# The first tile's opening of a two-layer decoder trunk, rebuilt: coefficients on VectorE, attention in batches, the merge in sections

## The chip, the cores and the metric

The kernel runs on one core of a Trainium2 chip. The metric is the time of one execution in device microseconds, as the median of several. Times inside the kernel come from one profiled execution, counted from its first instruction. DVE is VectorE, ACT is ScalarE, PE is TensorE (PEld its weight loads), POOL is GpSimd, SP is SyncE, which issues the plain DMAs; a DMA indexed by a tensor (a gather) is issued by GpSimd.

## What is computed

Two layers over 256 tokens of width 1024, float32. Each layer has a token mixer and a retrieval over single-neuron experts:

```python
h = rms_norm(x, g1); q, k, v, f, u_pool, u_ssm = split(h @ w_in)
att  = forgetting_attention(q, k, v, f)   # 8 heads x 64, q and k normalised, bias from cumsum(log_sigmoid(f))
pool = multiscale_pool(u_pool)            # windows 2, 4, 8, 16, then 64x64 products
ssm  = s5_mixer(u_ssm)                    # a_bar = exp(a*dt) complex, b_bar = (a_bar-1)/a*b, scan over time,
                                          # y = gelu(.), y * sigmoid(y @ glu_w + glu_b)
x = x + concat(rms_norm(att), rms_norm(pool), rms_norm(ssm)) @ w_out
h2 = rms_norm(x, g2)                      # PEER: for each of 8 heads, from h2 @ w_q:
                                          # top 16 of 128 keys, twice; top 16 of the 256 sums; softmax -> gates
act = gelu(h2 . u[expert])                # 128 experts a token
x = x + sum(gate * act * v[expert])
```

The outputs are the 256x1024 rows after both layers.

## The kernel before

Tokens are taken in tiles of 128, one token to a partition. Two tiles and two layers make four steps, n = 0 to 3 (n = 0 and 1 are the tiles of the first layer). In each step a token needs 128 expert rows (u and v side by side, 8 KB); expert E of all 128 tokens is one gather of 1 MB into one of 12 slots (`slot`). VectorE makes the dot product of u with h2 (`dots`), ScalarE the Gelu and, for each expert, a diagonal matrix with gate times Gelu (`weigh`), and TensorE adds diagonal times v into PSUM (`add_last`, one group behind). Four experts are a quad; a step has 32 quads. A gather into a used slot waits for `expert_done`.

Everything else is cut into pieces with names, and one list, `ORDER`, is walked by every engine, which takes from each name its own part. `MIX0` is the order ahead of the first gather: the whole mixer of step 0 up to its first routing head (`route0`), and of step 1 the projections up to q, k, v (entries `("qkv0", 1)`). Behind it `script()` deals rows of pieces to the quads: `ROUTES` (heads 1 to 7 of step 0) and `MIX1` (the rest of step 1's mixer and its eight routing heads) to the quads of step 0, and `MIX` with `ROUTES` of step n+1 to those of step n. `route` is, on VectorE, the top-16 work of one head, ending with the indices (`idx`, semaphore `routed`) and, after ScalarE's exponential, the gates.

The pieces that matter here: `dt`, `inverse`, `tab0` to `tab3` make the discretised coefficients of the state space model, on GpSimd, for one layer at a time: a Taylor polynomial (`exp_start`), nine squarings (`exp_double`), and `coefficients`; `tab4` makes the input matrices (`b_bar`), `rotate0` to `rotate2` tables of powers over time (for layer 1 on GpSimd, `tab5` to `tab7`). `bu`, `scan`, `backA`, `backB`, `y`, `z`, `glu` are the model itself: drive products, turning them by the powers, 16 scans along time, turning back, output, Gelu (here from Tanh on ScalarE and products on VectorE), gate. `qkn` normalises q and k, `qkT` transposes and scales them; `att0` to `att4` do two heads each: logits on TensorE into one half bank a head, `max` and `nrm` (maximum, and division by the sum) on VectorE for each head alone, exponential and copies on ScalarE. `attT`, `mixT` copy results out of PSUM, `sq`, `merge` compute the three norms together and `out0` to `out3` are the output projection; `x1` adds the residual.

The weights come in chunks of 1 MB. Those of step 0 up to `out3` lie in the 12 slots that later take experts; step 1 uses the same chunks for its projections, so a first gather waits until its slot's chunk is used by both. The other chunks pass through a ring of two buffers: chunk c is loaded when chunk c-2 is used, and the second buffer is scratch of step 0's model until `s_ready`.

## Time and profile before

| | |
|---|---|
| median of 3 runs | 1639.59 us (1638.54 to 1640.44) |
| profiled execution | 1639.44 us, span 1637.6 us |
| DVE busy | 1116.6 us (68%) |
| PE busy | 1079.0 us (66%) |
| POOL busy | 665.4 us (41%) |
| ACT busy | 431.1 us (26%) |
| DMA | 623.52 MB, of them 536.90 MB by gathers, mean 381 GB/s |
| mean granted TensorE clock | 0.825 of full speed |

The first gather is issued at 145.18 us. A busy share is a mean over stages that have different limits, so it says little by itself. The DMA row of the page has the mean busy share of the 16 DMA engines in 40 equal slices of 41 us; in the windows one sees the same for chosen stretches.

### The profile page before, as it was taken

The page shows a single profiled execution, that of the slowest core. Times are in us where ns is not written, and L with a number is a line of the kernel's source. Part 1 is how long each engine was busy: PE and PEld are TensorE (multiplying, and loading weights), DVE is VectorE, ACT ScalarE, POOL GpSimd, SP SyncE. Part 2 cuts the span into 40 slices and gives each one's busy share as a digit, 9 for nine tenths or more (in the row PEclk, how much of TensorE's full clock was granted, in tenths as well). Part 3 has the DMA queues.
Part 4 walks back from the last instruction along what each step waited for, and adds up shares of the span by engine and source line. Part 5 has one row for each costly group of instructions (what it writes and reads, how often), then busy time and mean ns, then how long its engine had stood idle before and what let it go on. Part 6 is the DMA issues. An engine that isn't in the chain of part 4 may idle for free. (4 is left out here: it accounts for less than half of the span.)

```text
span 1637.6 us, 19577 instructions
## 1 busy us (share of the span) xinstructions
PE 1079.0 (66%) x6936; PEld 560.8 (34%) x6936; DVE 1116.6 (68%) x2614; ACT 431.1 (26%) x1118; POOL 665.4 (41%) x793
## 2 busy tenths in 40 slices
PE   7795665777576576676677586667766656555654
PEld 6665331442343143332254243434244311111111
DVE  3833999755599957666379968656469975455455
ACT  2221332341233320234033331225133321111111
POOL 6002333685285344334433353344333354444431
PEclk9998786988788688888888797888878876787688
DMA  9005999979999899999999999999999999999997
GB/s 392 22 30 224 419 419 358 420 308 399 397 419 390 353 419 419 420 419 420 420 382 420 419 412 420 419 419 419 420 392 419 414 372 420 420 419 420 419 419 319
DMA packets 86067, 623.52 MB, mean 381 GB/s; under 512 B 9809, under 2 KB 9809, under 8 KB 10961
## 3 DMA queue, kind: packets, MB, share of 16 engines
q0 software_dynamic: 73728, 536.90, 79.8%
q1 hardware_dynamic: 12240, 85.37, 12.8%
q8 instruction: 54, 0.88, 0.2%
q14 instruction: 45, 0.36, 0.1%
HBM read 621.19 MB, written 1.05 MB: 380 GB/s over the span
## 5 line engine op out<-in xcount | busy, mean ns | idle before, releaser
L455 POOL DMA_INDIRECT slot<-experts,idx x512 | 570.5, 1114 | 928.6 <-PE acc L1348 722.4
L1038 DVE CUSTOM_DVE_ANT_0 slot<-slot,h 128x1024 f32<-128x1024 f32 x512 | 616.4, 1230 | 348.8 <-DMA slot<-experts,idx 337.5
L1348 PE MATMUL acc<-slot,diag 64*64 64x512 f32 x4080 | 612.3, 751 | 366.3 <-ACT diag L732 365.6
L1348 PEld LDWEIGHTS acc<-slot,diag 64*64 64x64 f32 x4080 | 179.2, 168 | 745.4 <-ACT diag L732 442.0
L732 ACT ACTIVATE diag<-cst,ge 128x64 f32<-128x64 f32 x510 | 136.2, 336 | 149.1 <-DVE ge L758 133.8
L723 ACT ACTIVATE ge<-ge 128x4 f32<-128x4 f32 x129 | 26.5, 206 | 475.5 <-DVE ge L1038 474.6
L1315 PE MATMUL PB<-hT,ring 128*128 128x128 f32 x1024 | 129.8, 289 | 14.1 <-DMA ring<-weights 9.8
L1315 PEld LDWEIGHTS PB<-hT,ring 128*128 128x128 f32 x1024 | 126.2, 205 | 16.7 <-issue 10.9
L723 ACT ACT_TABLE_LOAD x56 | 71.8, 1283 | 28.4 <-DVE ge L1038 27.5
L716 ACT ACTIVATE rs<-bs 128x1 f32<-128x1 f32 x32 | 6.5, 203 | 235.0 <-DVE bs L973 227.6
L1288 PE MATMUL PX<-ring,work 128*128 128x512 f32 x96 | 51.5, 686 | 16.7 <-DVE work L948 16.7
L1163 PE MATMUL PB<-ring,hT 128*128 128x256 f32 x192 | 51.8, 430 | 14.9 <-DVE work L758 14.9
L758 DVE TENSOR_TENSOR ge<-ge,gate 128x4 f32<-128x4 f32 x129 | 21.1, 164 | 48.4 <-ACT ge L723 17.5
L1163 PEld LDWEIGHTS PB<-ring,hT 128*128 128x128 f32 x192 | 40.8, 218 | 28.7 <-DVE work L758 16.6
L1038 DVE DVE_READ_ACCUMULATOR2_ANT ge<- 128x1 f32 x512 | 41.7, 82 | 0.0
L425 POOL TENSOR_TENSOR base<-base 128x16 f32<-128x16 f32 (+1 forms) x138 | 39.1, 301 | 4.6
L717 ACT ACT_TABLE_LOAD x31 | 39.8, 1283 | 0.6
L1288 PEld LDWEIGHTS PX<-ring,work 128*128 128x128 f32 x96 | 20.0, 219 | 48.0 <-issue 28.7
L668 ACT ACT_TABLE_LOAD x14 | 18.0, 1283 | 53.7 <-DVE att_s L922 53.6
L1299 PE MATMUL PB<-cst,h 128*128 128x128 f32 x32 | 7.2, 390 | 32.9 <-DVE h L962 32.8
L1213 PE MATMUL PX<-kT,qTz 128*128 128x128 f32 (+1 forms) x64 | 19.7, 396 | 11.1 <-DVE kT L909 11.1
L1324 PEld LDWEIGHTS PB<-ring,work 128*128 128x128 f32 x128 | 16.7, 190 | 26.3 <-issue 24.9
(227 smaller groups left out, 1143.7 us busy)
## 6 DMA issues: line engine op xcount, KB each, us to landing
ring<-weights SPq DMA_DIRECT2D x32, 1152.0 KB
ring<-weights SPq DMA_DIRECT2D x28, 1024.0 KB
slot<-weights SPq DMA_DIRECT2D x12, 1024.0 KB, 21.7
slot<-experts,idx POOLq DMA_INDIRECT x512
sml<-small SPq DMA_DIRECT2D x2, 1160.0 KB, 11.1
xs<-x SPq DMA_DIRECT2D x2, 512.0 KB, 7.8
out<-xs SPq DMA_DIRECT2D x4, 256.0 KB
cst<-consts SPq DMA_DIRECT2D x1, 564.5 KB, 4.7
```

The source lines that it names most:

```text
L425: return pool.tensor_tensor(o, a, b, op)
L455: pool.indirect_dma_start(out=slot[:, E % SLOTS, :], out_offset=None, in_=src, in_offset=bass.IndirectOffsetOnAxis(ap=idx[:, n % 2, e:e + ...
L717: told(act.activation(bs[:, 1, :], bs[:, 0, :], ACT.Exp, bias=rs[:, 0:1], accum_out=rs[:, 1:2]), "gexp_ready")
L723: act.activation(ge[:, 1, G % 2, :], ge[:, 0, G % 2, :], ACT.Gelu_apprx_tanh).then_inc(S["gelu_ready"], 1)
L732: act.activation(diag[:, d % DIAGS, :], c_("fold"), ACT.Copy, scale=ge[:, 2, G % 2, i:i + 1]).then_inc(S["diag_ready"], 1)
L758: return dve.tensor_tensor(o, a, b, op)
L1038: ins = dve.tensor_tensor_reduce(u, u, h2[:, n % 2, :], 1.0, 0.0, ALU.mult, ALU.add, d[:, i:i + 1])
L1163: ins = pe.matmul(PB[:, bank, (i % 2) * 256:(i % 2) * 256 + 256], hT_(n)[:, k, :], c[:, k, :], start=(k == 0), stop=(k == KD - 1))
L1213: pe.matmul(o, qTz[:, t, h // 2, h % 2, :], kT[:, h // 2, 0:w], start=True, stop=False)
L1288: ins = pe.matmul(PX[:, half, :], W[0][:, k * P:k * P + P], c[:, (k % 2) * D + half * 512:(k % 2) * D + half * 512 + 512], start=(k == 0), ...
L1315: ins = pe.matmul(PB[:, 2 + h % 2, i * P:i * P + P], c[:, k, i * P:i * P + P], hT[:, k, :], start=(k == 0), stop=(k == KD - 1))
L1348: ins = pe.matmul(acc[HALF * half:HALF * half + HALF, i, :], diag[rows, d % DIAGS, :], slot[rows, E % SLOTS, D + half * 512:D + half * 512 ...
```

## The change

`MIX0` is rewritten. The coefficients of both layers are made at once on VectorE (`power0` to `power2`, 16 columns instead of 8, imaginary part and real part in one operation where it goes), from a small table of their own (`factors`); `dt`, `inverse` and `tab0` to `tab3` of layer 1 disappear from step 0, where only `tab4` to `tab7` are left to GpSimd. Attention of step 0 is done in two batches of four heads (`logits`, `big`, `even`, `turn`, `pv`), the scan in three parts between them, norms and merge in three sections, pooling first, then attention, then the model (`sq1 merge1`, `sq0 merge0`, `sq2 merge2`), with the output chunks in the order 2, 0, 1, 3; results are read from PSUM without a copy. Gelu is one function of ScalarE. Queries lie unpadded in `qT`. The projections q, k, v of step 1 stand behind `route1`, and their normalisation and transposes are the first rows of the quads; `route1` is in `MIX0`. Experts go to slots in another order (`place`), the output chunks' slots first. In all steps the exponential of a routing head (`soft`) stands on ScalarE behind the quad's diagonals instead of ahead of them, and the product of Gelu and gate is four copies with a scale on ScalarE instead of one VectorE operation.

The core of the diff (places in PSUM and SBUF, renamings and packing on the host are left out):

```diff
-MIX0 = ("normA", "dt", "inverse", "tab0", "tab1", "tab2", "tab3", "tab4",
-        "normT", "u", "uT", "pf", "gate", "ln", "cum", ("normA", 1), "qkv0", "qkv1", ("normT", 1),
-        "rotate0", "qkv2", "qkv3", "qkn", "rotate1", "qkv4", "qkv5", "bT", "qkT", "v", "rotate2", "bu", "att0",
-        ("pf", 1), ("gate", 1), "pool", "max0", "scan", "nrm0", "mixp", "att1", ("u", 1), "backA", "mixT", "max1", ("ln", 1),
-        ("qkv0", 1), "backB", "nrm1", ("uT", 1), "att2", "max2", "y", "nrm2", ("qkv1", 1), "z", "att3",
-        "max3", "glu", ("cum", 1), "nrm3", ("qkv4", 1), "att4", "attT", "sq", "merge", ("qkv2", 1), ("qkv3", 1),
-        ("qkn", 1), "out0", "out1", "out2", ("qkT", 1), "out3", ("qkv5", 1), "x1", ("v", 1), "h2T", "rp",
-        "route0")
-MIX1 = (("bu",), ("scan",), ("backA",), ("backB",), ("y", "z"), ("glu", "pool", "dt", "inverse"),
-        ("att0", "max0", "nrm0"), ("att1", "max1", "nrm1", "mixp", "mixT"), ("att2", "max2", "nrm2", "tab0"),
-        ("att3", "max3", "nrm3", "tab1"), ("att4", "attT", "sq", "tab2"), ("merge", "tab3"),
+MIX0 = ("normA", "dt", "inverse", "normT", "u", "power0", "power1", "pf", "uT", "gate", "ln", "power2", "tab4",
+        "rotate0", "cum", ("normA", 1), "qkv0", "qkv1", "rotate1", ("normT", 1), "bT", "qkv2", "rotate2", "bu",
+        "qkv3", "qkn0", "scan0", "qkv4", "qkn1", "qkv5", "v", "qkT", "scan1", "logits0", "big0", "scan2", "logits1",
+        "big1", ("u", 1), "pool", "even0", ("pf", 1), "backA", ("uT", 1), "turn0", "even1",
+        ("gate", 1), "mixp", "pv0", "turn1", "backB", "pv1", ("ln", 1), "sq1", "merge1", "y", "z", ("cum", 1), "sq0", "merge0",
+        "glu", "out2", "out0", "out1", "sq2", "merge2", "out3", "x1", "h2T", "rp", "route0", "soft0",
+        "route1", "soft1", ("qkv0", 1), ("qkv1", 1), ("qkv2", 1), ("qkv3", 1), ("qkv4", 1), ("qkv5", 1))
+MIX1 = (("bu",), ("scan",), ("backA",), ("backB",), ("y", "z"), ("glu", "pool"),
+        ("att0", "max0", "nrm0"), ("att1", "max1", "nrm1", "mixp"), ("att2", "max2", "nrm2"),
+        ("att3", "max3", "nrm3"), ("att4", "sq"), ("merge",),
...
-            rows = [(0, r) for r in ROUTES] + [(1, r) for r in MIX1]
+            rows = [(1, r) for r in ((), ("qkn",), ("qkT", "v"))]
+            rows += [(0, r) for r in ROUTES[1:]] + [(1, r) for r in MIX1]
...
+            for step, row in rows[done:at]:
+                order += [("mix", "soft" + s[5:], step) for s in row if s[:5] == "route"]
...
+def place(E):
+    return (E + CH_OUT) % SLOTS
...
+def merged_by(n, i):
+    return 4 * n + ((2, 3, 1, 4)[i] if n == 0 else i + 1)
+def normed(n, sec=2):
+    return sec_order(sec) if n == 0 else 3 + n
+def sec_order(sec):
+    return (2, 1, 3)[sec]
...
                 if c == 1:
                     sp.wait_ge(S["s_ready"], 1)
+                    sp.wait_ge(S["chunk_used"], uses(0, CH_OUT + 2))
...
                     if E < SLOTS:
-                        pool.wait_ge(S["chunk_used"], max(uses(0, E), uses(1, E) if in_slot(1, E) else 0))
-                        pool.wait_ge(S["qkT_ready"], 2)
+                        i = place(E)
+                        pool.wait_ge(S["chunk_used"], max(uses(0, i), uses(1, i) if in_slot(1, i) else 0))
...
-                if part == 0:
-                    exp_start(l)
-                elif part == 1:
-                    exp_double(l, HALVINGS // 2)
-                elif part == 2:
-                    exp_double(l, HALVINGS - HALVINGS // 2)
-                elif part == 3:
-                    coefficients(l)
-                elif part == 4:
+                if part == 4:
                     b_bar(l)
...
+                    return
+                if part == 5:
+                    pool.wait_ge(S["states_ready"], TILES)
+                rotate(l, tt, lag, link, W[1], ((1, 2, 4, 8, 16), (32,), (64,))[part - 5])
...
+                act.preload_act_table_set("natural_log_exp_and_others")
+                told(act.activation(step[:, :], tabc[:, 2, :], ACT.Exp), "dt_ready")
...
+                act.preload_act_table_set("natural_log_exp_and_others")
...
-                told(act.activation(gl[:, 1, :, :], gl[:, 0, :, :], ACT.Tanh, scale=GELU_S), "gtanh_ready")
+                told(act.activation(gl[:, 0, :, :], gl[:, 2, :, :], ACT.Gelu_apprx_tanh), "z_ready")
...
+            def logits(n, a):
+                act.wait_ge(S["nmax_ready"], 4 * a + 4)
+                for i in range(4):
+                    at = 4 * a + i
+                    told(act.activation(W[2][:, at * P:at * P + P], PX[:, a, i * P:i * P + P], ACT.Exp,
+                                        bias=att_s[:, 0, at:at + 1], accum_out=att_s[:, 1, at:at + 1]), "exp_ready")
+            def turn(n, a):
+                act.wait_ge(S["probT_psum"], 4 * a + 4)
+                told(act.copy(W[2][:, a * 512:a * 512 + 512], PB[:, a, :]), "probT_ready", 4)
...
+            def sq(n, sec=None):
...
+            def merge(n, sec=None):
+                act.wait_ge(S["norm_psum"], normed(n, 2 if sec is None else sec))
+                cols = slice(0, 3 * P) if sec is None else slice(sec * P, sec * P + P)
+                told(act.activation(rB[:, :, :].rearrange("p a b -> p (a b)")[:, cols], norm_at(n)[:, cols], ACT.Sqrt,
                                bias=eps), "norm_rms")
...
+            def soft(n, h):
+                R = PH * n + h
                 act.wait_ge(S["top_ready"], R + 1)
                 link(act.activation(rs[:, 0:1], bs[:, 0, 0:1], ACT.Copy, scale=-1.0))
                 told(act.activation(bs[:, 1, :], bs[:, 0, :], ACT.Exp, bias=rs[:, 0:1],
...
+                if quad % PER_HEAD == 0 and quad < QUADS:
+                    act.wait_ge(S["gated"], PH * n + quad // PER_HEAD + 1)
+                for i, E in enumerate(mine):
+                    e = E - PICKS * n
+                    ins = act.activation(ge[:, 2, G % 2, i:i + 1], ge[:, 1, G % 2, i:i + 1], ACT.Copy,
+                                         scale=gate[:, n % 2, e:e + 1])
+                told(ins, "w_ready")
...
+            def power(n, part):
+                if part == 0:
+                    dve.wait_ge(S["zeroed"], 1)
+                    dve.wait_ge(S["dt_ready"], 1)
+                    lag(stt(zz[:, 0, 0, :], tabc[:, 0, :], 0.5 ** HALVINGS, step[:, :], ALU.mult, ALU.mult))
+                    link(stt(zz[:, 1, 1, :], tabc[:, 1, :], 0.5 ** HALVINGS, step[:, :], ALU.mult, ALU.mult))
...
+                    for k in range(TERMS - 1, 0, -1):
+                        lag(stt(A, Z, 1 / k, U[:, 0, :].unsqueeze(1).to_broadcast(wide), ALU.mult, ALU.mult))
+                        link(stt(B, Z, 1 / k, U[:, 1, :].unsqueeze(1).to_broadcast(wide), ALU.mult, ALU.mult))
+                        lag(stt(U[:, 0, :], A[:, 0, :], 1.0 if k > 1 else 0.0, B[:, 1, :], ALU.add, ALU.subtract))
+                        link(tt(U[:, 1, :], A[:, 1, :], B[:, 0, :], ALU.add))
+                elif part == 1:
+                    for i in range(HALVINGS):
+                        x, y = ((U, A), (A, U))[i % 2]
+                        p, q = ((U, B), (B, U))[i % 2]
+                        lag(stt(A[:, 0, :], x[:, X[i % 2], :], 2.0, x[:, X[i % 2], :], ALU.add, ALU.mult))
+                        lag(stt(B[:, 0, :], p[:, 1, :], 4.0 ** i, p[:, 1, :], ALU.mult, ALU.mult))
+                        lag(stt(q[:, 1, :], x[:, X[i % 2], :], 1.0, p[:, 1, :], ALU.add, ALU.mult))
+                        link(tt(y[:, X[1 - i % 2], :], A[:, 0, :], B[:, 0, :], ALU.subtract))
+                else:
+                    R, pr, pi = ta[:, 1, 0, :], ta[:, 1, 1, :], tb[:, 1, 1, :]
...
+                    e = ta[:, 0, :, :]
+                    pair = [P, 2, LSB]
+                    lag(tt(uu[:, 0, :, :], e, tabc[:, 0, :].unsqueeze(1).to_broadcast(pair), ALU.mult))
+                    link(tt(tb[:, 0, :, :], e, tabc[:, 1, :].unsqueeze(1).to_broadcast(pair), ALU.mult))
+                    lag(tt(drive_c[:, 0, :], uu[:, 0, 0, :], tb[:, 0, 1, :], ALU.add))
+                    link(tt(drive_c[:, 1, :], uu[:, 0, 1, :], tb[:, 0, 0, :], ALU.subtract))
...
+            def scan(n, part=3):
...
+                if part % 3 == 0:
+                    link(tt(w3[0], w3[0], spare, ALU.add))
+                    link(tt(w3[1], w3[1], w3[3], ALU.subtract))
+                for r in ((), (0,), (1,), (0, 1))[part]:
...
-                link(dve.tensor_scalar(gl[:, 0, :, :], gl[:, 0, :, :], GELU_C, 1.0, ALU.mult, ALU.add))
-                told(tt(gl[:, 0, :, :], gl[:, 0, :, :], y, ALU.mult), "garg_ready")
-            def z(n):
-                gl = gl_(n)
-                y = gl[:, 2, :, :]
-                dve.wait_ge(S["gtanh_ready"], n + 1)
-                told(dve.scalar_tensor_tensor(gl[:, 0, :, :], gl[:, 1, :, :], 1.0, y, ALU.add,
-                                         ALU.mult), "z_ready")
+                told(ins, "yd_ready")
...
-                qp, kp = (b.rearrange("p (a b) -> p a b", a=PAIRS) for b in qk_banks(n)[1:])
-                for o in range(2):
-                    r = slice(64 * o, 64 * o + 64)
-                    link(dve.tensor_scalar(qTz[r, t, :, o, :], qp[r], s_("qg")[r], DH ** -0.5, ALU.mult, ALU.mult))
...
+                link(dve.tensor_scalar(qT[:, t, :, :], qp, s_("qg"), DH ** -0.5, ALU.mult, ALU.mult))
...
+            def big(n, a):
+                dve.wait_ge(S["logits_psum"], 4 * a + 4)
+                told(dve.tensor_reduce(att_s[:, 0, 4 * a:4 * a + 4], PX[:, a, :].rearrange("p (h k) -> p h k", h=4), AX.X,
+                                       ALU.max, negate=True), "nmax_ready", 4)
+            def even(n, a):
+                dve.wait_ge(S["exp_ready"], 4 * a + 4)
+                link(dve.reciprocal(att_s[:, 2, 4 * a:4 * a + 4], att_s[:, 1, 4 * a:4 * a + 4]))
+                x = W[2][:, a * 512:a * 512 + 512].rearrange("p (h k) -> p h k", h=4)
+                told(tt(x, x, att_s[:, 2, 4 * a:4 * a + 4].unsqueeze(2).to_broadcast([P, 4, P]), ALU.mult),
+                     "prob_ready", 4)
...
-            def attT(n):
-                dve.wait_ge(S["pv_psum"], HEADS * (n + 1))
-                told(dve.tensor_copy(h2[:, n % 2, 0:512], PB[:, 2, :]), "attT_ready")
...
+            def merge(n, sec=None):
+                dve.wait_ge(S["norm_rms"], normed(n, 2 if sec is None else sec))
+                secs = slice(0, 3) if sec is None else slice(sec, sec + 1)
+                link(dve.reciprocal(rB[:, secs, :], rB[:, secs, :]))
+                for k in range(KD) if sec is None else BLOCKS[sec]:
...
-                        ins.then_inc(S["merged_ready"], 1)
-                dve.wait_ge(S["merged_ready"], 4 * (n + 1))
+                        told(ins, "merged_ready")
...
-                if G >= 2:
-                    dve.wait_ge(S["diag_ready"], by_tensor(experts_of(*divmod(G - 2, QUADS))[-1] + 1))
-                told(tt(w, ge_(1, n, quad), gate[:, n % 2, mine[0] - PICKS * n:mine[-1] + 1 - PICKS * n], ALU.mult),
-                     "w_ready")
...
+                    pe.wait_ge(S["hT_ready"], 4)
+                if n == 1:
+                    pe.wait_ge(S["v_ready"], 2)
+                    pe.wait_ge(S["qkT_ready"], 2)
...
                 if n == 1 and i == 0:
-                    pe.wait_ge(S["up_ready"], 2)
-                    pe.wait_ge(S["fx_ready"], 2)
-                if n == 1 and i == 2:
-                    pe.wait_ge(S["attT_ready"], 1)
+                    pe.wait_ge(S["x1_ready"], 1)
                 if n == 1 and i == 4:
-                    pe.wait_ge(S["sig_ready"], 1)
-                bank = qk_banks(n)[0] + i // 2
+                    pe.wait_ge(S["h2T_ready"], 2)
...
+            def logits0(n, a):
...
+                for i in range(4):
+                    one_head(n, 2 * i + a, PX[:, a, i * P:i * P + P], P)
+            def turn0(n, a):
+                pe.wait_ge(S["prob_ready"], 4 * a + 4)
+                for i in range(4):
+                    at = 4 * a + i
+                    ins = pe.transpose(PB[:, a, i * P:i * P + P], W[2][:, at * P:at * P + P], ident)
+                ins.then_inc(S["probT_psum"], 4)
+            def pv0(n, a):
+                pe.wait_ge(S["probT_ready"], 4 * a + 4)
+                if a == 0:
+                    pe.wait_ge(S["uT_ready"], 2)
+                for i in range(4):
+                    h, at = 2 * i + a, 4 * a + i
+                    ins = pe.matmul(PB[DH * a:DH * a + DH, 2, i * P:i * P + P], V[:, 0, h * DH:(h + 1) * DH],
+                                    W[2][:, at * P:at * P + P], start=True, stop=True)
+                ins.then_inc(S["pv_psum"], 4)
...
+            def merge(n, sec=None):
+                pe.wait_ge(S["sq_ready"], normed(n, 2 if sec is None else sec))
+                if n == 0 and sec != 1:
+                    pe.wait_ge(S["norm_rms"], normed(n, sec) - 1)
+                for i in range(3) if sec is None else (sec,):
+                    sq = sq_at(n, i)
...
+                pe.wait_ge(S["merged_ready"], merged_by(n, i))
+                if n == 0:
+                    pe.wait_ge(S["exp_ready"], HEADS)
```

## Rows read from the trace of the kernel before

**Rows 1.** Page, part 2: what DMA moved in 40 equal slices.

```profile
GB/s 392 22 30 224 419 419 358 420 308 399 397 419 390 353 419 419 420 419 420 420 382 420 419 412 420 419 419 419 420 392 419 414 372 420 420 419 420 419 419 319
```

**Rows 2.** Waits: who waited for whom, us in total, times, longest.

```profile
POOL slot L455 <- DVE idx L1010: 106.4, 1, 106.4
```

**Rows 3.** Windows: length, busy us and instructions by engine, clock, DMA.

```profile
core 0: us, PE busy (x) PEld busy (x) DVE busy (x) ACT busy (x) POOL busy (x), PEclk, DMA share, GB/s
260.00:300.00 40.00, 23.25 (x162) 7.43 (x163) 38.58 (x71) 5.63 (x22) 19.88 (x16) 0.75 0.94 376
340.00:380.00 40.00, 24.74 (x148) 12.61 (x148) 22.00 (x44) 12.71 (x30) 33.20 (x67) 0.80 0.78 295
500.00:580.00 80.00, 47.30 (x312) 20.86 (x312) 73.83 (x198) 29.14 (x69) 36.20 (x34) 0.77 0.93 370
900.00:1265.00 365.00, 252.26 (x1680) 134.46 (x1680) 262.01 (x600) 110.49 (x275) 138.60 (x124) 0.83 1.01 416
```

**Rows 4.** Timeline, from the residual to the first indices: start, length, instruction.

```profile
123.82 1.22 DVE L758 TENSOR_TENSOR xs<-xs,PX 128x1024 f32<-128x1024 f32 x1 [1.11 <-PE PX L1288]
...
144.71 0.17 DVE L1010 SCALAR_TENSOR_TENSOR idx<-ex 128x16 uint32<-128x16 f32 x1
```

**Rows 5.** Groups by form, 0 to 145 us: busy us, mean ns, idle before.

```profile
L1163 PE MATMUL PB<-slot,h 128*128 128x256 f32 x96 | 22.6, 391 | 0.8 <-ACT ring L629 0.8
L1163 PE MATMUL PB<-slot,hT 128*128 128x256 f32 x96 | 21.2, 380 | 0.0
...
L1288 PE MATMUL PX<-slot,work 128*128 128x512 f32 x32 | 14.1, 592 | 0.0
...
L1112 PE MATMUL PB<-slot,h 128*128 128x256 f32 x16 | 5.4, 510 | 5.8 <-DVE work L758 5.8
...
L1112 PE MATMUL PX<-slot,hT 128*128 128x256 f32 x16 | 3.6, 379 | 0.0
```

**Rows 6.** Windows of VectorE's work on the tile rot: length, busy, instructions.

```profile
32.00:40.00 8.00, 6.86 (x31) 1.00 1.02 420
43.00:46.00 3.00, 2.10 (x6) 1.00 0.06 25
49.00:53.20 4.20, 3.70 (x6) 1.00 0.01 4
```

**Rows 7.** Timeline of the opening, six kinds of work on VectorE and GpSimd.

```profile
33.28 0.27 DVE L758 TENSOR_TENSOR work<-rot 128x8 f32<-128x8 f32 x2
...
34.24 2.88 POOL L425 TENSOR_TENSOR ring<-tabp,base 128x256 f32<-128x256 f32 x4
...
37.20 1.53 POOL L425 TENSOR_TENSOR ring<-ring 128x256 f32<-128x256 f32 x2
...
55.96 2.48 DVE L758 TENSOR_TENSOR work<-PB,rot 128x1024 f32<-128x1024 f32 x2
...
61.64 5.16 DVE L846 TENSOR_TENSOR_SCAN work<-base,work 128x128 f32<-128x128 f32 x16
...
103.45 2.55 DVE L943 RECIPROCAL rB<-rB 128x384 f32<-128x384 f32 x1 [6.64 <-ACT rB L686]
```

**Rows 8.** Timeline of ScalarE around one table load.

```profile
25.07 1.28 ACT L613 ACT_TABLE_LOAD   x1
...
26.37 0.40 ACT L613 ACTIVATE work<-work,cst 8x128 f32<-8x128 f32 x1
```

**Rows 9.** Timeline of one quad with a routing head, late in step 0.

```profile
507.59 1.22 DVE L1038 CUSTOM_DVE_ANT_0 slot<-slot,h 128x1024 f32<-128x1024 f32 x1
...
512.29 0.49 DVE L969 MAX8 ts<-work 128x8 f32<-128x128 f32 x2
...
514.33 3.74 PE L1315 MATMUL PB<-hT,ring 128*128 128x128 f32 x32
...
520.73 1.06 ACT L732 ACTIVATE diag<-cst,ge 128x64 f32<-128x64 f32 x4 [0.70 <-DVE ge L758]
```

**Rows 10.** Timeline of GpSimd: first and last of 108 arithmetic instructions.

```profile
316.51 0.12 POOL L472 MEMSET base<- 128x8 f32 x1
...
370.24 0.24 POOL L521 TENSOR_SCALAR base<-base 128x8 f32<-128x8 f32 x1
```

More of the change, by code:

```diff
@@ L733, in weigh @@
                                    scale=ge[:, 2, G % 2, i:i + 1]).then_inc(S["diag_ready"], 1)
-            run(dict(dt=dt, normA=normA, gate=gate, ln=ln, bT=turn_b, z=z, glu=glu, qkn=qkn, v=v, att=att, pool=pool_, sq=sq,
-                     merge=merge, x1=x1_, h2T=h2T, rp=rp, route=route), lambda n, quad: None, weigh)
+            run(dict(dt=dt, normA=normA, gate=gate_, ln=ln, bT=turn_b, z=z, glu=glu, qkn=qkn, v=v, att=att, pool=pool_, sq=sq,
+                     logits=logits, turn=turn,
+                     merge=merge, x1=x1_, h2T=h2T, rp=rp, route=route, soft=soft), lambda n, quad: None, weigh)
         @block.vector
```

447 lines of the change are left out of this document (218 added, 229 removed), and 4 rows, old and new, of the table MIX.

## The prediction

> **What bounds the kernel now.** I read the slices of the page first. What DMA moves is near 420 GB/s in all slices but numbers two to four: the queue is busy for the first 40 us, almost empty until the gathers begin, and then full to the end [rows 1]. So the kernel is an opening of 145 us with little traffic and 1,490 us of expert rows. Only two things can change the time: when the first gather is issued, and how much DMA stands still later. The waits say the first: GpSimd's gather waits 106.4 us, once, for the first indices [rows 2]. The windows of 40 us say the second [rows 3]; a loss is the GB/s missing to 420, over 420, times the length. 260 to 300 loses 4.2 us, 340 to 380 loses 11.9, 500 to 580 loses 9.5; 900 to 1265 stands for the rest with 1%. The losses look different: at 260 to 300 and 500 to 580 VectorE is busy 96 and 92% of the time, at 340 to 380 only 55%, while GpSimd has 67 instructions and 33 of 40 us.
>
> **The opening.** Today the first indices are written at 144.88 [rows 4]. Twelve q, k, v chunks of TensorE stand ahead of that; the six of tile 1, 22.6 us, leave [rows 5]. VectorE loses there tile 1's key and query normalisation and scaling and much waiting between heads. What is left has to be laid on the engines anew.
>
> *To 22.2 us.* Nothing changes until the first tile's hT at 11.5. Then VectorE raises the powers in 67 narrow operations. Two such take 0.27 together [rows 7]; with pipelining I take 0.1 for one that waits only for the one before last and 0.2 for one whose own end is awaited: 3.0 us (10 and 10), 4.5 (27 and 9) and 1.5 (7 and 4), with 1.6 for uT between them. GpSimd then has only the B matrices left, 4.5 us as today (34.24 to 38.73 [rows 7]), to 26.8.
>
> *To 51.6.* rotate0 takes 7.3 as now, 31 operations, of them 6.86 busy, beside GpSimd [rows 6]; cum, normA and hT 0.7, 0.9 and 1.45; rotate1 and rotate2 2.1 and 3.9 [rows 6]: 38.6. Turning the drive: four operations of 1.24 [rows 7], 43.6. Then qkn's reduction, two sums and qkn's product, again over 1024 columns: 5.3, to 48.8. TensorE's own sum, with six chunks of 3.65 (between the 3.53 and 3.77 of the rows), ends at 48.7, a tie; from here a slower TensorE costs one for one. Transposes 1.1 and two scalings 1.5: 51.6.
>
> *To 68.1.* VectorE: sixteen scans 5.2 [rows 7], two maxima over 512 columns 1.3, even0 and even1 0.85 each, backA and backB 3.7 and 4.1, uT 0.4: 68.1. TensorE meanwhile: logits 3.9, u of tile 1 3.9, pool 0.8, pf of tile 1 5.5, so the batched turn starts at 65.8, 7 us after its probabilities, and the last value product ends at 69.8. Both arms end within 2 us.
>
> *To 91.2.* Here ScalarE's tables set the pace. merge1's root costs 1.28+0.28; VectorE stands before it until 72.9, then does 1.5 (a third of the 2.55 reciprocal [rows 7] and two products of 0.3). y 0.6; Gelu 1.28+0.42, to 76.9; squares 0.6, norm sum 0.7 and glu product 1.2, to 79.5; a root and a tanh, each behind its load, to 81.8; glu 0.4; out0 and out1 1.75 each (0.44 for a 512-column matmul [rows 5]), to 85.7, out2 being hidden. The last section: sum 0.4, root 1.56, merge2 1.5, out3 1.75, with 0.3 of hand-overs 91.2. From x1 to the indices the chain is today's: 123.82 to 144.88, 21.1 us [rows 4]. Sum 112.4.
>
> **TensorE's clock.** Rows show what a restart costs: pf's 16 matmuls took 5.4 us after 5.8 us of idling and 3.6 without it [rows 5], 1.8 us. The new order has sparse work before out2. I add one such restart (bounds: pf itself warm, 110.6; three, 117.8) and forecast the first indices at 114: 31 us earlier, bounds 27 and 34.
>
> The trace shows a table load as 1.28 us with 0.02 to its operation [rows 8]. The Trainium skill, "ScalarE: Activation LUTs", section "What ACT_TABLE_LOAD costs", puts about 1.38 us of drain on top of each switch, and that speaks against this change. By that figure the five switches on the chain would make 114 into 121. The rows show no such time, and I take none.
>
> **The head start behind it.** On TensorE the second tile's q, k, v now stand behind route1, and gathers 6 to 11 need those chunks' slots. TensorE comes to them some 1 us after the indices and frees one each 3.65: at +4.6 up to +22.9. DMA needs 2.5 us a gather (1 MB at 420 GB/s), and has six free ones, 5.6 us of landing latency and two weight chunks ahead: gather 11 is served at about +35. This cover is 12 us; without it each us is one of DMA. Behind the waiting gather on GpSimd's queue stand only later gathers. SP's second ring chunk now also waits for out2, at 81, and is needed at 105. route1 on VectorE, 8.2 us (512.29 to 520.5 [rows 9]), moves out of the crowded stretch to where VectorE waits for the first expert.
>
> **Step 0 after that.** (a) GpSimd's arithmetic for layer 1, 108 instructions from 316.51 to 370.48 [rows 10], is gone; it stood in blocks of 6 to 12 us before groups of four gathers that carry 10 us. VectorE has room there: -12 (bounds -13, and -5 if another engine limits). (b) 260 to 300: VectorE now lacks route1's 8.2 and gets tile 1's normalisation, 5.0: -4.2 (bounds that and 0). (c) At the end of step 0, 34 rows are dealt to 32 quads; eight routes fall on seven quads, the last with two. A quad with a route is 4.9+8.2 on VectorE (dots from 507.59, maxima from 512.29 [rows 9]) against 12.8 on DMA (4 MB and 1.15 MB of weights): eight routes in eight quads leave VectorE 2.5 us short (105 for 102.4), eight in seven 7.5 (99.9 for 92.4). In return diagonals no longer wait for the route's end: they come at 520.73 though the dots end at 512.25, and could come at 515.5; TensorE's other work ends at 518.07 [rows 9], so slots are free 3 us sooner, each time, and VectorE may fall 3 us further behind. In the last quad the exponential of route6 stands behind route7's copy and comes some 4 us late. Net 5+4-3 = +6 (bounds -4, where the 3 us count in every quad and the 4 not, and +10).
>
> (d) Four small ScalarE copies, 0.2 us each like its narrow operations, replace one VectorE product of a quad. ScalarE is 26% busy (the table), so they are hidden while slots come in time. In steps 1 to 3 I take 0 (bounds -4 and +5). At the very end one dependent operation more: +0.2.
>
> **Sum.** The profiled execution took 1639.4 (span 1637.6; median of the runs 1639.6): 1639.4-31-12-4.2+6+0.2 = 1598.4.
>
> **Rivals.**
> *Only the opening pays*: 340 to 380 was spare, and the crowded end takes all back: 1639.4-31 = 1608.4. For it: VectorE at 92% in 500 to 580 [rows 3]. Against: 45% of room at 340 to 380. 0.20.
> *The opening is a chain of hand-overs* that costs 8 more, indices at 122: 1606.4. For it: some 20 hand-overs between 68 and 91, and the restart's row. Against: today's hand-overs, 0.1 each, are in my sum. 0.12. By the skill's drain alone, part of this case, it would be 1605.3, 0.04 of it.
> *Slots come sooner everywhere*: (c) is -4 and the later steps give 3: 1585.4. For it: the 3 us of earlier diagonals. Against: throughput of VectorE, not latency, limits there. 0.14.
> *Slower.* One mechanism: the route's exponential stands on ScalarE behind the quad's diagonals, and the third of these waits for TensorE's products. Gelu, copies and diagonals end about 3.9 us after the dots, the exponential at 6.4, VectorE wants it at 7.7: 1.3 us in hand. If it is later than that by 2.9 us at each of the 14 routes of step 0, where VectorE is the limit, 41 us are lost and the gain is gone; at 3.2 the time is 1643. Against: TensorE is ahead, its products for the next quad's route ran from 514.33 [rows 9], 11 us before VectorE's maxima could use them. 0.02.
> *The change does nothing*, another wait holding the first gather: 1639, 0.01. The forecast itself: 0.51.
>
> **The numbers.** 1598.4 is the likeliest, its own range 1592 to 1604. Terms' bounds and the rivals' reach give 1586 to 1611 for eight in ten. What a measurement can tell from no change here is 0.2%, 3.3 us. Faster 0.96, same 0.015, slower 0.025.
>
> **What would show it.** Right: the first gather near 114; the powers' operations ending near 22; pf of tile 1 straight ahead of the batched turn; five table loads between 71 and 88; no dip at 300 to 350, one at the end of step 0. Wrong: the first gather before 108 or after 120; gathers 6 to 11 issued after DMA ran dry; VectorE waiting for ScalarE's exponential in each route; the dip of 340 to 380 back under another releaser.

## The result and the profile after

The changed kernel took 1617.77 us (median of 4 runs, 1612.66 to 1619.6) against 1640.01 for the kernel before: ratio 0.9857, 95% interval 0.9835 to 0.988. I had forecast 1598.4 with a range of 1586 to 1611. It is faster, as said, but by little more than half of what was said.

The profiled execution's span is 1614.6, 23.0 less. This splits at the first indices. Waits of the changed kernel (who waited for whom, us in total, times, longest):

```profile
POOL slot L521 <- DVE idx L1097: 117.0, 2, 113.7
ACT rs L750 <- DVE bs L1060: 30.8, 29, 6.4
```

and its timeline at the first indices (start, length, instruction):

```profile
141.12 0.17 DVE L1097 SCALAR_TENSOR_TENSOR idx<-ex 128x16 uint32<-128x16 f32 x1
```

They come at 141.29. Before it was 144.88 [rows 2, 4]: only 3.6 us earlier, where I forecast 31. The other 19.4 us came behind the opening, where I forecast 10.0. Both halves were wrong, in opposite directions. The split is good to some 2 us only: one profiled execution stands for each kernel, and six kernels below that keep the old opening (e6, e7, e8, e11, e12, e13) have their first indices between 142.3 and 143.4.

**Where the opening lost it.** My working held to within 1.7 us as far as the scaled queries and keys (ready at 51.6 by the sum; the first logit starts at 53.34). Then the timeline of TensorE shows the first head of the batched logits, the first product of the fifth, and what follows the eighth:

```profile
53.34 0.48 PE L1299 MATMUL psum<-kT,qT 64*128 64x128 f32 x2 [1.70 <-DVE kT L991]
53.76 0.49 PE L1300 MATMUL psum<-cT,cst 128*128 128x128 f32 x2
54.08 0.39 PE L1301 MATMUL psum<-cst,cT 128*128 128x128 f32 x2
54.31 0.39 PE L1302 MATMUL psum<-cst 128*128 128x128 f32 x2
...
60.91 0.79 PE L1299 MATMUL psum<-kT,qT 64*128 64x128 f32 x2
...
69.97 0.42 PE L1185 MATMUL psum<-h,slot 128*128 128x128 f32 x1
```

The first head takes 1.28 us, the second 1.7, the later ones 2.30, and all eight 16.6 (53.34 to 69.97) where I had put 3.9. The windows of 5 us (columns as in [rows 3]) show why they change in mid-stream:

```profile
50.00:55.00 5.00, 2.75 (x18) 2.19 (x18) 3.67 (x9) 0.00 (x0) 0.00 (x0) 1.00 0.01 3
...
65.00:70.00 5.00, 5.00 (x20) 4.10 (x20) 0.00 (x0) 0.00 (x0) 0.00 (x0) 0.50 0.00 0
...
90.00:95.00 5.00, 0.00 (x0) 0.00 (x0) 2.92 (x7) 2.52 (x5) 0.00 (x0) 0.50 0.00 0
95.00:100.00 5.00, 4.71 (x18) 4.15 (x19) 0.79 (x1) 2.73 (x4) 0.00 (x0) 0.52 0.00 0
```

The granted clock is 1.00 at 50 and down to 0.50 from about 55.5 to 72, with TensorE busy all the time from the first logit on. Before the logits it had idled twice, 1.24 us ahead of the transposes and 1.70 behind them. It falls again at 90 to 100, this time behind idling. From the merge to the routing the timeline has:

```profile
95.29 2.08 PE L1396 MATMUL psum<-work,cst 128*128 128x128 f32 x8 [5.40 <-ACT work L696]
...
98.86 4.06 PE L1407 MATMUL psum<-slot,ring 128*128 128x512 f32 x8
102.76 7.03 PE L1407 MATMUL psum<-slot,work 128*128 128x512 f32 x16
...
113.74 5.23 PE L1407 MATMUL psum<-slot,work 128*128 128x512 f32 x8 [3.50 <-DVE work L1036]
```

Two output chunks are 16 instructions and 7.03 us, so one is 3.5. I had read [rows 5] as 1.75.

**Where the rest gained.** Windows from the first indices to the end of each step, the kernel before first, then the changed one:

```profile
144.00:566.00 422.00, 267.13 (x1776) 137.54 (x1775) 331.19 (x861) 127.77 (x316) 223.71 (x297) 0.81 0.96 387
566.00:947.00 381.00, 254.55 (x1716) 136.50 (x1720) 271.28 (x640) 111.72 (x282) 141.73 (x127) 0.84 1.01 415
947.00:1325.00 378.00, 262.44 (x1760) 140.34 (x1752) 272.81 (x640) 113.66 (x284) 145.22 (x130) 0.83 1.00 411
```

```profile
141.00:556.00 415.00, 279.72 (x1874) 154.31 (x1872) 326.59 (x822) 151.70 (x441) 195.61 (x191) 0.83 0.98 402
556.00:928.00 372.00, 255.32 (x1724) 135.34 (x1724) 264.09 (x606) 138.66 (x412) 146.05 (x128) 0.84 1.00 415
928.00:1305.00 377.00, 267.38 (x1748) 143.27 (x1748) 265.34 (x599) 140.55 (x412) 143.80 (x128) 0.83 1.01 416
```

Step 0 was 33 us short of a full queue (422 times 33/420) and is now 20 short (415 times 20/422). Step 1's 9 us are no better use of the queue, 415 both times: bytes moved from it into step 0, whose transfers run further ahead. And the full rate itself is another: 419 to 420 GB/s in [rows 1], here mostly 421:

```profile
GB/s 391 30 30 239 422 420 422 407 315 422 411 420 420 357 412 422 421 420 421 421 392 421 421 421 421 421 416 420 421 382 421 421 411 421 421 421 421 422 421 310
```

What is new in step 0 is one dip. Windows of the changed kernel around it, and GpSimd's next gather in its timeline:

```profile
260.00:300.00 40.00, 20.84 (x124) 5.79 (x116) 39.28 (x67) 9.28 (x31) 18.87 (x15) 0.70 1.01 421
320.00:340.00 20.00, 13.12 (x53) 7.92 (x56) 9.22 (x23) 6.17 (x19) 1.49 (x2) 0.57 0.62 258
340.00:380.00 40.00, 30.58 (x229) 15.47 (x222) 24.64 (x46) 23.05 (x62) 21.37 (x20) 0.95 0.98 398
```

```profile
339.43 0.94 POOL L521 DMA_INDIRECT slot<-experts,idx  x1 [18.51 <-PE psum L1463]
```

The gather waits 18.5 us for a slot, at clock 0.57, while the second tile's attention begins. The dip of [rows 3] at 260 is gone, and that at 340 nearly (398 GB/s for 295).

### The profile page after: what moved, and what is told of

Read it like the earlier page. It is cut to its first block and busy times, and to the rows that moved or that the text cites. A ratio compares the mean times of both kernels' runs of the same rounds, so it can differ in the third digit from the quotient of the medians.

```text
span 1614.6 us, 19582 instructions
## 1 busy us (share of the span) xinstructions
PE 1089.5 (67%) x6936; PEld 570.1 (35%) x6936; DVE 1091.3 (68%) x2504; ACT 539.2 (33%) x1626; POOL 626.1 (39%) x577
## 5 line engine op out<-in xcount | busy, mean ns | idle before, releaser
L1463 PE MATMUL psum<-slot,diag 64*64 64x512 f32 x4080 | 598.4, 736 | 319.5 <-ACT diag L773 312.4
L1463 PEld LDWEIGHTS psum<-slot,diag 64*64 64x64 f32 x4080 | 175.1, 165 | 689.4 <-ACT diag L773 371.7
L1430 PE MATMUL psum<-hT,ring 128*128 128x128 f32 x1024 | 136.7, 298 | 24.1 <-DMA ring<-weights 18.7
L1430 PEld LDWEIGHTS psum<-hT,ring 128*128 128x128 f32 x1024 | 132.9, 214 | 27.2 <-issue 20.2
L764 ACT ACTIVATE ge<-ge,gate 128x1 f32<-128x1 f32 x512 | 109.0, 283 | 4.2
L1407 PE MATMUL psum<-ring,work 128*128 128x512 f32 x96 | 50.5, 675 | 18.1 <-DVE work L1036 18.1
L1245 PE MATMUL psum<-ring,hT 128*128 128x256 f32 x192 | 50.9, 424 | 12.3 <-DVE work L803 12.3
L1245 PEld LDWEIGHTS psum<-ring,hT 128*128 128x128 f32 x192 | 40.1, 215 | 25.9 <-DVE work L803 14.1
L1407 PEld LDWEIGHTS psum<-ring,work 128*128 128x128 f32 x96 | 19.6, 216 | 49.0 <-issue 28.3
L1439 PE MATMUL psum<-ring,work 128*128 128x128 f32 x128 | 23.3, 306 | 9.3 <-ACT work L736 9.3
L1439 PEld LDWEIGHTS psum<-ring,work 128*128 128x128 f32 x128 | 17.1, 194 | 33.8 <-issue 19.7
```

What stands on the lines that cost most here:

```text
L764: ins = act.activation(ge[:, 2, G % 2, i:i + 1], ge[:, 1, G % 2, i:i + 1], ACT.Copy, scale=gate[:, n % 2, e:e + 1])
L1245: ins = pe.matmul(bank[:, (i % 2) * 256:(i % 2) * 256 + 256], hT_(n)[:, k, :], c[:, k, :], start=(k == 0), stop=(k == KD - 1))
L1407: ins = pe.matmul(PX[:, half, :], merged(n, k), c[:, (k % 2) * D + half * 512:(k % 2) * D + half * 512 + 512], start=(k == (4 if n == 0 el ...
L1430: ins = pe.matmul(PB[:, 2 + h % 2, i * P:i * P + P], c[:, k, i * P:i * P + P], hT[:, k, :], start=(k == 0), stop=(k == KD - 1))
L1439: ins = pe.matmul(PB[:, 2 + h % 2, 256 + i * P:256 + i * P + P], qTs[:, h % 2, i * P:i * P + P], raw[:, KD * 256 + i * P:KD * 256 + i * P ...
L1463: ins = pe.matmul(acc[HALF * half:HALF * half + HALF, i, :], diag[rows, d % DIAGS, :], slot[rows, place(E), D + half * 512:D + half * 512 ...
```

## Experiments on the opening

Median, ratio to the kernel before with its 95% interval, end of the first indices in the profiled execution. The kernels were run in groups at different times, each beside runs of the kernel before (whose medians were 1638.4 to 1641.4), so between groups the ratios are the better comparison.

| kernel | us | ratio | indices |
|---|---|---|---|
| changed | 1617.8 | 0.9857 (0.9835 to 0.988) | 141.3 |
| e1: grouped by shape | 1610.5 | 0.9831 (0.9815 to 0.9848) | 134.4 |
| e2: padded queries | 1608.7 | 0.9826 (0.9809 to 0.9842) | 132.2 |
| e3: before, unpadded | 1639.2 | 1.0004 (0.999 to 1.0018) | 143.8 |
| e4: grouped, v in the gap | 1615.3 | 0.9857 (0.9841 to 0.9873) | 140.0 |
| e9: padded, kept warm | 1599.2 | 0.9762 (0.9729 to 0.9795) | 124.9 |
| e10: e9, two pieces moved | 1597.5 | 0.9738 (0.9717 to 0.9759) | 124.1 |

**e1, logits grouped by shape.** Here and in e4 the sums of four heads are open in one bank at the same time, and the values are left out of account; only the time counts.

```
-for i in range(4): one_head(n, 2 * i + a, PX[:, a, i * P:i * P + P], P)
+for i in range(4): matmul(o[i], qT[rows, 0, i], kT[rows, i, 0:P], start=True)   # 64 rows
+for i in range(4): the three 128-row matmuls of head 2 * i + a
```

> The changed kernel, but in the batched logits the four products of 64 rows (query by key) of a half come first and the twelve of 128 rows (decays and mask) behind them, so that TensorE changes between the two shapes twice in place of eight times. Theory 1, the changes of shape make the logits long (16.6 us for 8 heads, where the kernel before took 0.88 us a head) and the clock falls because of them: the logits take 5 to 7 us, the first indices come 9 to 12 us earlier (129 to 132 us) and the time is 1606 to 1609. Theory 2, the clock falls by itself at this place and the change of shape is cheap: the logits stay over 12 us and the time within 2 us of the changed kernel's 1617.8. Theory 3, the opening's end is set by something else (SP's or POOL's queue): logits shorter, indices still at 141.

**e2, padded queries.** `qTz[P, TILES, PAIRS, 2, P]`, zeroed once, and two scalings as in the kernel before; the product reads `qTz[:, t, h // 2, h % 2, :]` and `kT[:, h // 2, 0:w]`.

> The changed kernel with the queries padded with zeros to 128 rows, as in the kernel before, so that every product of the logits has 128 rows; the order within a head is that of the changed kernel. Costs one VectorE operation more after the transposes (about 0.5 us). Theory 1, the changes of shape are the cost: logits 5 to 7 us, first indices at 129 to 133, time 1606 to 1610, and steps 1 to 3 change by a microsecond at most, since attention there is hidden. Theory 2, not the shape but the batching or the clock: logits over 12 us and the time at 1617 to 1620.

e2 has its logits in 7.2 us, its indices at 132.2 and 1608.7 us: theory 1, with the logits a little over its 5 to 7. e1 (logits 9.4 us, 54.67 to 64.09; 134.4; 1610.5) goes theory 1's way but misses its three ranges by 1.5 to 2.4 us. The timeline of TensorE in e2, the first head, a later one, and what follows:

```profile
54.46 0.49 PE L1302 MATMUL psum<-kT,qTz 128*128 128x128 f32 x2 [2.49 <-DVE kT L994]
54.78 0.39 PE L1303 MATMUL psum<-cT,cst 128*128 128x128 f32 x2
...
60.81 0.39 PE L1302 MATMUL psum<-kT,qTz 128*128 128x128 f32 x2
...
61.70 3.74 PE L1188 MATMUL psum<-h,slot 128*128 128x128 f32 x32
```

A head is 0.90 us to the last, the clock stays at 1.00, and the first indices come 9.1 us earlier. The time is 9.1 us lower by the medians and 5.1 by the two ratios. In e1 the clock fell too, but came back within the batch. The 5 us from 55 on, in e1, in e2 and in e10 (padded as well, described below):

```profile
55.00:60.00 5.00, 5.00 (x31) 4.78 (x30) 2.28 (x8) 0.00 (x0) 0.00 (x0) 0.66 0.00 0
```

```profile
55.00:60.00 5.00, 5.00 (x47) 5.00 (x46) 3.60 (x11) 0.75 (x4) 0.00 (x0) 1.00 0.00 0
```

```profile
55.00:60.00 5.00, 5.00 (x33) 5.00 (x32) 2.01 (x6) 0.00 (x0) 0.00 (x0) 0.66 0.00 0
```

So padding doesn't rule the fall out. The idle times ahead of the batch were 1.70 us in e1, 2.49 in e2, and in e10 2.49 with another 1.23 ahead of the transposes; e10's logits took 8.9 us (53.85 to 62.73). What lets the clock fall at this place, idling or the 64-row products, stays open. What the three have against the changed kernel is that the clock was at 1.00 again from 59 on, while there, with the two shapes alternating, it stayed at 0.50 to the end of the batch.

**e3, the kernel before with unpadded queries alone.** `qT` for `qTz`, one scaling for two, `qT[rows, t, h // 2, :]` in the product.

> The kernel before with only its queries unpadded (64 rows in the query by key product, one VectorE operation less), the rest of the change left out. Theory 1: a head's four products go from 0.88 us to 1.3 to 2.3 us, eight of them +3 to +11 us on TensorE, of which the waits between heads hide a part: first indices 2 to 6 us later than 144.9 and the time 1642 to 1646. Theory 2, the shape is cheap: 1639 to 1641 and a head at 0.9 us.

Theory 2 on the time, theory 1 on the price of a head. A head is now 1.28 us (in the timeline the first starts at 49.68 and the second at 50.96), 0.38 more than padded, but at full clock, two heads at a time, with waits of TensorE between the pairs that hide it. The same edit is free in the old order and costs 9 us of the first indices in the batch.

**e4, v of the second tile in TensorE's gap.** Grouped logits, and `("qkv4", 1), ("qkv5", 1)` ahead of the pooled section's sum of squares.

> As the grouped logits, and the second tile's v (two of its six projections and the copy) is moved from behind the first tile's routing into TensorE's idle stretch ahead of the merge. Theory A, the cold clock in the merge (0.5 granted between 90 and 100 us) costs some 4 to 6 us and work in the gap keeps it up: indices 2 to 5 us earlier than with the grouped logits alone, time 1601 to 1606. Theory B, the filled work only stands in front of the merge: indices the same or 1 to 2 us later, time within 2 us of the grouped kernel's.

Theory B, and worse than it said: 4.8 us slower than e1, indices 5.5 later. The attention section's sum of squares starts at 92.59 where e1 has 88.20, so the two chunks stand in front of the merge; the clock falls all the same further down (the last output chunk 6.57 us, the first routing product 6.75). This doesn't settle what the clock costs; the next run does.

**e9, padded and kept warm.**

```
+def warm(n, times):
+    for i in range(times):
+        pe.matmul(PB[:, 1, :], ident, cst[:, 0:512], start=True, stop=True)
 ... "pv1", "warm2", ... "y", "z", "warm5", ... "merge2", "warm3", "out3", "warm4", "x1"
```

> The changed kernel with padded queries, and 14 products of 128 by 512 whose result nobody reads, in four places where TensorE stands idle in the opening (2 behind the last value product, 5 behind the state output, 3 behind the third sum of squares, 4 behind the last output projection; 0.88 us each at full clock). With padded queries alone the first indices came at 132.1, and three stretches ran at half clock: the first heads' sum of squares 2.07 us, the last output projection 5.36, the first routing product 6.23. Theory A, the falls of the clock cost their sum, 1.2 + 1.8 + 2.5 = 5.5 us: those three at 0.9, 3.6 and 3.8 us, indices at 126 to 128, time 1602 to 1605. Theory B, the products stand in the way or the clock falls all the same: indices at 131 to 134 and the time within 2 us of 1608.7.

Theory A, and more: 7.3 us, not 5.5. In the timeline of e9 the three that ran cold (2.07, 5.36 and 6.23 us in e2) are

```profile
85.37 1.16 PE L1403 MATMUL psum<-work,cst 128*128 128x128 f32 x8 [1.02 <-ACT work L697]
...
101.67 3.70 PE L1414 MATMUL psum<-slot,work 128*128 128x512 f32 x8 [0.92 <-DVE work L1039]
...
111.55 3.84 PE L1437 MATMUL psum<-hT,ring 128*128 128x128 f32 x32 [0.73 <-ACT hT L727]
```

with the granted clock at 1.00 in every window from 45 to 125. They make 5.0 of it. The glu product (1.06 for 1.92), the first output chunk (3.60 for 4.31) and the transposes (1.44 for 1.89) make 2.0 more, and e9's logits started 0.4 us earlier than e2's, which its edit doesn't explain. So the warm clock is worth 7.0.

**e10, e9 with two pieces moved.** `("ln", 1), ("cum", 1)` to behind `"out1"`, `"sq2", "merge2"` ahead of it, `"warm2"` and `"warm3"` dropped. Nine unread products are left, not the 11 of the text below.

> The changed kernel with padded queries, 11 of the 14 unread products, and two pieces of the opening moved: the second tile's forget gate (a ScalarE table load of 1.28 us and two activations, and VectorE's scan) from ahead of the pooled section's root to behind the last sum of squares, and the gated section's sum of squares ahead of the second attention projection in place of behind it. Worked out from the padded and warmed run: its root, reciprocal and scaling (4.1 us after the sum) come to lie beside a projection of 3.5 us, -3.3, and the pooled section's squares no longer wait 2.0 us for the gate, -2. Theory A, the opening is one chain: indices at 119 to 121 in place of 124.9, time 1593 to 1596. Theory B, what is moved is replaced by the next waits: indices at 123 to 125 and the time within 2 us of 1599.2.

Theory B by both numbers (124.1, and 1.7 us below e9), though something did move: the last output chunk ends at 101.7, 3.7 us earlier than in e9 (of 5.3 expected), but the first indices come only 0.8 earlier. The timeline of e10:

```profile
104.26 1.28 ACT L583 ACT_TABLE_LOAD   x1
105.56 0.29 ACT L583 ACTIVATE st<-st,cst 128x1 f32<-128x1 f32 x1
...
109.13 5.47 PE L1437 MATMUL psum<-hT,ring 128*128 128x128 f32 x32 [0.73 <-ACT hT L727]
```

The gate's logarithm, moved behind the last root, leaves another table on ScalarE, and the root of x1 loads its own: 1.28. The routing product is cold again: 1.6. 3.7 - 1.3 - 1.6 = 0.8. The 1.6 that the 3.7 lack are about what the fall of the clock in e10's own logits cost: they end 1.5 us later than e9's, and so does the last value product. It is the fastest kernel here, with intervals that overlap e9's.

## Experiments behind the opening

| kernel before, with | us | ratio |
|---|---|---|
| e6: gate product on ScalarE, softmax behind the weights | 1627.9 | 0.9929 (0.9907 to 0.9951) |
| e8: gate product on ScalarE alone | 1634.7 | 0.9972 (0.9956 to 0.9989) |
| e7: no layer 1 powers on GpSimd | 1627.1 | 0.9925 (0.9897 to 0.9953) |
| e13: e6 and e7 | 1615.5 | 0.9851 (0.9833 to 0.9868) |
| e11: buffers 96 bytes further | 1637.1 | 0.9984 (0.9971 to 0.9996) |
| e12: buffers 24 bytes further | 1636.1 | 0.9981 (0.9968 to 0.9993) |

**e6 and e8, ScalarE's edits.**

```
 act Gelu; told "gelu_ready"
+wait "gated"; 4 x activation(ge[:, 2, G % 2, i:i+1], ge[:, 1, G % 2, i:i+1], Copy, scale=gate[...]); told "w_ready"
-(dve) w = ge1 * gate
 e6 only: route() ends after rp(); soft() = negation and exponential, placed behind ("close", n, quad)
```

> The kernel before with two of the change's edits alone, those to the steady phase on ScalarE: the gate product as four ScalarE copies in place of one VectorE product, and the softmax of a routing behind the expert weights of its quad. The opening and GpSimd's arithmetic stay. Some 17 us of the changed kernel's gain come after its first indices. Theory P, as predicted: these edits are worth nothing and GpSimd's arithmetic was the cost: 1636 to 1641. Theory Q, the diagonals no longer wait for VectorE (365.6 us of TensorE's idle time ended with one before), so slots come free sooner: 1618 to 1630.

> The kernel before with the gate product alone as four ScalarE copies; the softmax stays ahead of the expert weights on ScalarE. Tells the two ScalarE edits apart. Theory P: 1636 to 1641. Theory Q, if the gain is the missing hand-over to VectorE and back: most of the other run's gain, 1622 to 1632. Theory R, if it is the place of the softmax (its wait for VectorE's sorting holds the diagonals up): little of it, 1634 to 1641.

Theory Q for both together (e6), 11.7 us by the ratio where I had forecast nothing; theory R for e8, so more of it (7 us) is the softmax's place than the product (4.6). The two intervals only just stay apart. ScalarE's waits for VectorE's top values in the kernel before, in e8 and in e6:

```profile
ACT rs L716 <- DVE bs L973: 227.6, 31, 21.5
```

```profile
ACT rs L716 <- DVE bs L978: 220.3, 32, 21.8
```

```profile
ACT rs L722 <- DVE bs L984: 21.4, 29, 1.1
```

In e8 ScalarE stands up to 21.8 us in this wait with the diagonals of the quad behind it. With the softmax behind them it doesn't. The softmax can't be moved alone: VectorE's product would wait behind a routing that waits for the softmax.

**e7, GpSimd's arithmetic.** `tab` parts 0 to 2 of the second layer left out and part 3 cut to its one signal (steps 2 and 3 run with the first layer's numbers).

> The kernel before with GpSimd's arithmetic for the second layer's coefficients left out (the exponential's series, the doublings and the combination; the first layer's numbers are used in steps 2 and 3, so that only the time counts). The rotation tables and the input matrix are still made. Theory P, as predicted: the arithmetic keeps VectorE and the issue of gathers waiting and costs 5 to 13 us, middle 12: 1625 to 1633. Theory Q: it lies beside work that waits for transfers: 1635 to 1640.

Theory P, at its middle: 12.3 us. Windows of e6, which keeps the arithmetic, and of e7, over the stretch of [rows 3, 10]:

```profile
340.00:380.00 40.00, 24.87 (x132) 11.16 (x128) 21.21 (x40) 15.29 (x41) 30.30 (x61) 0.74 0.85 325
```

```profile
340.00:380.00 40.00, 30.82 (x190) 12.28 (x192) 26.80 (x52) 14.01 (x34) 18.02 (x18) 0.87 1.01 419
```

**e13, both.**

> The kernel before with the gate product on ScalarE, the softmax behind the expert weights, and GpSimd's arithmetic for the second layer left out (first layer's numbers used in steps 2 and 3). Alone the first two gave 11.7 us of the medians, and the last 12.3; what the change gained behind its first indices is about 19. Theory A, they act on different stretches and add: 1614 to 1619. Theory B, both relieve the same stretches (what the queue loses between 240 and 380 us): 1619 to 1624.

Theory A: they add, 12.3 + 11.7 against 24.4 (interval 21.6 to 27.4). Its windows:

```profile
143.00:550.00 407.00, 258.77 (x1769) 134.40 (x1767) 327.87 (x829) 157.37 (x445) 187.44 (x192) 0.82 0.99 403
550.00:926.00 376.00, 254.06 (x1724) 135.29 (x1724) 266.35 (x608) 139.62 (x411) 144.36 (x128) 0.84 1.01 417
926.00:1305.00 379.00, 262.42 (x1748) 143.41 (x1748) 268.62 (x609) 141.51 (x411) 141.15 (x128) 0.84 1.00 414
```

With the old opening it is as fast as the changed kernel. Its step 0 takes 407 us and the changed kernel's 415. Only about half of those 8 us are lost: step 0 is 15.5 us short of a full queue here (407 times 16/419) and 19.7 there, and the rest are bytes that the changed kernel moves ahead of step 1 (372 us for 376). The 4 us are put down to the fuller step 0 (second tile's normalisation, q, k and v, 34 rows in 32 quads); no run has it alone.

**e11 and e12, the address.** `pad = sb("pad", [P, 24])` or `[P, 6]` ahead of `ring`.

> The kernel before with 96 unused bytes a partition ahead of its ring and expert buffers, so that these lie at the addresses that they have in the changed kernel. Nothing else. The full-queue rate is 419 to 420 GB/s in the kernel before and in those of its variants, and 421 to 422 in the changed one and all of its variants, which is 0.4% of 1470 us, 5 to 7 us. Theory A, the address: 421 to 422 GB/s and 1632 to 1636. Theory B, the rate comes of what the engines do (less VectorE or GpSimd work beside the transfers, no chunk of the ring moved differently): 419 to 420 GB/s and 1637 to 1642.

> The kernel before with 24 unused bytes ahead of the ring and expert buffers, which puts them at a multiple of 64 bytes within a partition (of the buffers' summed sizes: 34664 bytes before, 34688 here, 34760 in the changed kernel). Theory A, the address sets the rate: 421 to 424 GB/s, 1628 to 1636. Theory B: 419 to 420 GB/s and 1637 to 1642.

Theory A on the rate, less on the time. The slices of e11:

```profile
GB/s 395 21 29 247 421 419 353 423 293 403 398 419 391 355 421 420 422 420 422 422 400 420 421 417 422 421 421 421 422 365 421 412 376 421 422 421 421 421 421 313
```

Mostly 421 and 422 where [rows 1] has 419 to 420, with nothing else changed; e12 has mostly 421. The four other variants of the kernel before in this table and e3 have 419 to 420, all variants of the changed one mostly 421. The gain is 2.6 us by the ratio in e11 and 3.1 in e12, below the 5 to 7 expected. Where the rest of it goes no run shows. Both intervals exclude 1, but the single times overlap with those of the kernel before.

## Why the prediction was wrong

**First indices, forecast 114, measured 141.3.** The step that failed is "*To 68.1*", at "logits 3.9", and then the chunks:

| term | forecast | measured | from |
|---|---|---|---|
| logits, all at 128 rows and full clock | 3.9 | 7.2 | e2 |
| the 64-row product, 0.38 us a head | 0 | 3.0 | e3, 8 x (1.28 - 0.90) |
| half clock in the batch | 0 | 6.4 | 16.6 - 8 x 1.28 |
| out0, out1, out3 | 3 x 1.75 | 3 x 3.5 | timeline |
| clock from the merge on | 1.8 | 7.0 | e9 against e2 |

The surplus is 3.3 + 3.0 + 6.4 + 5.3 + 5.2 = 23.2 of 27.3. In the other 4.1 are the queries' 1.7 us up to 53.3 and a table load of 1.28 for the second tile's logarithm, which I had not counted. The first and fourth terms are plain sizing. No row gives the 3.9: it is what four heads take, not eight, at the 0.9 to 1.0 us that a padded head has in the kernel before and in e2. And a 512-column product of this type is two instructions, [rows 5] gives 14.1 us for four chunks, and I halved it. The second and third were no term at all. The unpadded queries stood in the change and got no price, and I took the clock for something that falls behind idling and is back after one piece of work; here it stayed at half through 14 us of busy TensorE.

**Rival "a chain of hand-overs".** Its time (1606.4) was nearer to the measured one, but not for its reason. The hand-overs themselves were as I counted them: in e9, where TensorE is warm, the root of the attention section, the table load and the tanh follow each other within 0.1 us. The Trainium skill, "ScalarE: Activation LUTs", section "What ACT_TABLE_LOAD costs", would put a drain of about 1.38 us on each load. Here the load at 104.26 in e10 ends at 105.54 and its root starts at 105.56: the drain isn't seen, and the measurement decides.

**(a) GpSimd's arithmetic, -12.** Right: 12.3 in e7, in the place named.

**(b) 260 to 300, -4.2.** The dip is gone (376 to 421 GB/s), as forecast; no run has it alone.

**(c) The end of step 0, +6.** The number is about met, by luck: step 0 lost some 4 us against e13, which has (b) in it too, but not where I said. 500 to 580 lost 9.5 us before, 7.8 in e13 (378 GB/s against 419) and 7.2 in the changed kernel (384 against 422), so the two routes in the last quad cost nothing that shows. What is lost is the new dip at 320 to 340, 7.8 us (20 times 164/422) where e13 has 418 GB/s; there the 64-row logits of the second tile run at half clock. With padded queries a dip stays: in e2 the ten microseconds from 320 run at 175 GB/s, 5.9 us lost. So the shape isn't its whole cause, and the rest of it was not settled.

**(d) ScalarE's copies and "steps 1 to 3 I take 0".** Failed in size, where I had put 0 with a bound of -4: 11.7 us. I had priced the four copies by ScalarE's busy share (each took 0.28 us, not 0.2: 109.0 us for 512; e8, which has them alone, is 4.6 us faster all the same), and the earlier diagonals only as three us at each route, of which VectorE took most back. The wait of 227.6 us for the top values stood in the profile; at it I should have asked what was queued behind it, as I did for the exponential. The slower rival, the exponential coming late, did not show: VectorE's waits of the changed kernel have none for the exponential.

**Not foreseen at all: the address**, 3 us.

**The sum behind the opening.** From the first indices to the end the profiled executions take 1492.7 us before, 1472.7 in e13 and 1473.3 in the changed kernel. So e13's edits give 20.0 there (24.4 by the ratio, for the whole), the address 3, and the fuller step 0 takes some 4: 19.0, against 19.4 measured. This adds up runs that were never made together, each good to 2 or 3 us. The forecast was 10.0. So 27.3 too much in the opening and 9.4 too little behind make the 18 us by which the spans' difference (23.0 for 41) fell short; that the range was missed by only 7 us is owed to the gain that I hadn't foreseen.

## What to carry to other kernels

Count the instructions of a product in the profile before halving it, and price a batch of matmuls by what one group of the same shapes took at both clocks: work that is free between waits is on the path once it is batched. When a wait is long, ask what is queued behind the waiting instruction, however idle its engine is. Where TensorE waits in a serial stretch, cheap products that nobody reads can pay: 14 of them gave 9.5 us here by the medians, more than the opening as it was first rebuilt gave at the first indices (3.6).

## What the runs showed of the hardware

- A 64-row matmul among 128-row ones cost 0.38 us a head at full clock (1.28 for 0.90, e3 and e2). Eight such heads back to back ran at half clock from the third on, with TensorE busy throughout (16.6 us). Padded to 128 rows they took 7.2 us at 1.00 in e2 and e9, and 8.9 in e10, where the clock was at 0.50 from 55 to 58.4 and then came back within the batch. Grouped (two changes of shape for eight) they took 9.4. Why the clock stays down in the mixed batch, the rows per product or the gaps at each change, and what starts the fall, stay open; a batch of 64-row products alone was not run.
- The full rate of the expert transfers depended on where the buffers lie in a partition: 419 to 420 GB/s with the expert buffers at an offset of 34664 bytes (by the tiles' summed sizes), mostly 421 to 422 at 34688 and at 34760 (e12, e11).
- 14 unread products in waits kept TensorE's clock at 1.00 over 80 us (45 to 125, e9) in which e2's fell three times. With 9 of them (e10) it fell at the logits and again at the first routing product.
